# Norms' sums as products with a matrix of ones: root and reciprocal on 256 columns, no spread

## The reference, cut to what matters

```python
EPS = 1e-6
def rmsnorm(x, g):
    xf = x.astype(jnp.float32)
    y = xf * lax.rsqrt(jnp.mean(xf * xf, axis=-1, keepdims=True) + EPS)
    return (y * g.astype(jnp.float32)).astype(x.dtype)
```

## Time and profile before

| | |
|---|---|
| median of three runs | 2409.51 us |
| the profiled execution | 2409.11 us |
| its span | 2407.3 us |
| mean granted clock of TensorE | 0.988 |
| TensorE busy | 98% |
| VectorE busy | 81% |
| ScalarE busy | 63% |
| mean DMA rate | 259 GB/s |

### The profile page before, as it was taken

The page is one execution under the profiler, slowest core; times in us unless marked ns, Lnnn a source line. Parts: engine busy times, 40 slices in busy tenths (PEclk is TensorE's granted clock), DMA queues, the critical chain, the costliest instruction groups (busy, mean ns, idle before and its releaser), DMA issues.

```text
span 2407.3 us, 39686 instructions
## 1 busy us (share of the span) xinstructions
PE 2355.6 (98%) x14994; PEld 2023.5 (84%) x14994; DVE 1944.8 (81%) x2671; ACT 1519.8 (63%) x2074; POOL 0.8 (0%) x6
## 2 busy tenths in 40 slices
PE   8999999999999999999999999998999999999998
PEld 7999999999877777777777777776999999999998
DVE  6756877986588998989898989897796877887664
ACT  5655443545477878878787878786645553645552
POOL 0000000000000000000000000000000000000000
PEclk9999999999999999999999999999999999999999
DMA  9443778545579998989898999997323668323440
GB/s 370 166 155 141 291 299 340 216 192 228 210 272 357 343 366 334 366 335 364 336 363 336 365 342 358 354 352 299 140 106 131 223 241 332 141 106 141 178 156 18
DMA packets 88271, 623.69 MB, mean 259 GB/s; under 512 B 9764, under 2 KB 11464, under 8 KB 13384
## 3 DMA queue, kind: packets, MB, share of 16 engines
q1 hardware_dynamic: 87600, 621.28, 67.8%
q10 hardware_dynamic: 536, 0.53, 0.1%
HBM read 620.72 MB, written 1.05 MB: 258 GB/s over the span
## 4 chain that ended last, share of the span: by engine, by line
PE 90%; DVE 5%; ACT 2%; issue 1%; DMA 0%; SPq 0%; ACTq 0%; DVEq 0%
PE bank L653 14%; PE bank L655 14%; PE bank L654 14%; PE bank L673 10%; PE bank L677 10%; PE bank L674 10%; PE bank L874 3%; PE bank L873 3%; PE bank L871 3%; DVE ring_r L1707 2%; PE bank L1072 1%; PE bank L1218 1%; PE bank L1083 1%; DVE ring L1692 1%; PE bank L982 1%
## 5 line engine op out<-in xcount | busy, mean ns | idle before, releaser
L1707 DVE TENSOR_TENSOR ring_r<-ring,ring_r 128x1024 fp32r<-128x1024 f32 x402 | 489.5, 1222 | 183.2 <-ACT ring_r L1295 182.7
L1295 ACT ACTIVATE ring_r<-ring 128x1024 fp32r<-128x1024 f32 x402 | 423.1, 1056 | 306.9 <-PE bank L677 134.3
L673 PE MATMUL bank<-XH,ring_r 128*128 128x256 f32 x2000 | 493.0, 284 | 1.8 <-DVE ring_r L1707 1.8
L674 PE MATMUL bank<-XH,ring_r 128*128 128x256 f32 x2000 | 490.6, 283 | 0.0
L2174 DVE TENSOR_TENSOR ring_r<-ring,Z_r 128x1024 fp32r<-128x1024 f32 x336 | 409.1, 1224 | 44.8 <-ACT Z_r L1549 44.7
L2174 DVE TENSOR_TENSOR ring_r<-ring,mhat_r 128x1024 fp32r<-128x1024 f32 x336 | 406.5, 1220 | 35.3 <-ACT mhat_r L1549 34.0
L1549 ACT ACTIVATE Z_r<-ring 128x1024 fp32r<-128x1024 f32 x336 | 355.0, 1060 | 100.1 <-PE bank L655 100.0
L1549 ACT ACTIVATE mhat_r<-ring 128x1024 fp32r<-128x1024 f32 x336 | 355.2, 1061 | 89.4 <-PE bank L655 86.3
L673 PEld LDWEIGHTS bank<-XH,ring_r 128*128 128x128 f32 x2000 | 383.7, 192 | 3.1 <-DVE ring_r L1707 2.6
L674 PEld LDWEIGHTS bank<-XH,ring_r 128*128 128x128 f32 x2000 | 383.8, 192 | 0.1
L654 PE MATMUL bank<-ring_r,xn_r 128*96 128x512 f32 x896 | 351.6, 392 | 0.0
(11 more groups left out here) (351 smaller groups left out, 3638.3 us busy)
## 6 DMA issues: line engine op xcount, KB each, us to landing
ring<-in_experts SPq DMA_DIRECT2D x336, 1024.0 KB, 6.8
ring<-in_stream SPq DMA_DIRECT2D x245, 1024.0 KB, 7.3
ring<-in_stream SPq DMA_DIRECT2D x8, 512.0 KB, 6.1
xT<-in_xT SPq DMA_DIRECT2D x2, 512.0 KB, 4.6
mhat<-in_memT SPq DMA_DIRECT2D x1, 1024.0 KB, 16.7
swap<-in_early SPq DMA_DIRECT2D x1, 1024.0 KB, 19.2
swap<-in_late SPq DMA_DIRECT2D x1, 1024.0 KB, 10.2
out_T<-xn SPq DMA_DIRECT2D x8, 128.0 KB, 2.0
```

The lines of the kernel that those rows point to most:

```text
L673: pe.matmul(dst, hi[:, a], x_hi(kb), start=(n == 0), stop=False)
L674: pe.matmul(dst, lo[:, a], x_hi(kb), start=False, stop=False)
L1295: act.activation(wh(Q), raw(Q), ACT.Copy).then_inc(sems["whi"], 1)
L1707: dve.tensor_tensor(raw(Q, ring_r), raw(Q), wh(Q).bitcast(F32), ALU.subtract).then_inc(sems["wlo"], 1)
```

## The change

The sums are products with a matrix of ones as weights and the squares as the moving operand, one product of 256 columns for each block instead of two of one column. The result is in 256 columns on all partitions at once. Root and reciprocal run on 128x256, in a new tile `rroot`, and `norm_apply` reads that tile instead of a bank. The spread and its bank are gone from the plan. Norm 6 keeps the columns, norm 8 its own form. Of the filling products of the exposed norms, two stand before the sums and two behind the root; the one before the spread is gone.

```diff
+        rroot = sb("rroot", [P, 2, S])
...
         G.plan("nrm0", 1)
-        G.plan("spread0", 1)
...
         def plan_ffn(i, ni):
             G.plan(f"nrm{ni}", 1)
-            G.plan(f"spread{ni}", 1)
...
-                    for t in range(NT):
-                        mm = pe.matmul(bank[G.bank(key)][:, t:t + 1], sqb(i, kb)[:, t * P:(t + 1) * P], ones[:, 0:1],
-                                       start=(n == 0 and t == 0), stop=(kb == KB - 1), skip_group_check=True)
-                G.filled(mm, key)
-
-            def norm_spread(i):
-
-                key = f"spread{i}"
-                G.wait_free(pe, key)
-                if i in EXPOSED:
-                    keep_busy(key, 1)
-                W(pe, "rc", i)
-                for t in range(NT):
-                    mm = pe.matmul(bank[G.bank(key)][:, t * P:(t + 1) * P], rcol[:, i % 2, t:t + 1].to_broadcast([P, P]),
-                                   ident, start=True, stop=True)
+                    if i == 6:
+                        for t in range(NT):
+                            mm = pe.matmul(bank[G.bank(key)][:, t:t + 1], sqb(i, kb)[:, t * P:(t + 1) * P], ones[:, 0:1],
+                                           start=(n == 0 and t == 0), stop=(kb == KB - 1), skip_group_check=True)
+                    else:
+                        mm = pe.matmul(bank[G.bank(key)][:, 0:S], ones, sqb(i, kb), start=(n == 0), stop=(kb == KB - 1))
                 G.filled(mm, key)
                 if i in EXPOSED:
-                    G.wait_drained(pe, f"nrm{i}")
-                    keep_busy(f"nrm{i}", 2)
+                    G.wait_drained(pe, key)
+                    keep_busy(key, 2)
...
-            proj_f("f.u", 0, "f.u", between=lambda m: norm_spread(1) if m == 2 else None)
+            proj_f("f.u", 0, "f.u")
...
-                G.drained(act.activation(rcol[:, i % 2, :], bank[G.bank(key)][:, 0:NT], ACT.Sqrt, scale=1.0 / D, bias=eps),
-                          key)
+                dst, n = (rcol[:, 0, :], NT) if i == 6 else (rroot[:, i % 2, :], S)
+                G.drained(act.activation(dst, bank[G.bank(key)][:, 0:n], ACT.Sqrt, scale=1.0 / D, bias=eps), key)
...
-                dve.reciprocal(rcol[:, i % 2, :], rcol[:, i % 2, :]).then_inc(sems["rc"], 1)
-
-            def norm_apply(i, src=xT, dst=xn, hold=False):
-                key = f"spread{i}"
-                G.wait_full(dve, key)
-                g = gcol(i)
+                r = rcol[:, 0, :] if i == 6 else rroot[:, i % 2, :]
+                dve.reciprocal(r, r).then_inc(sems["rc"], 1)
+
+            def norm_apply(i, src=xT, dst=xn):
+                if i == 8:
+                    G.wait_full(dve, "spread8")
+                else:
+                    W(dve, "rc", i)
+                r, g = bank[G.bank("spread8")][:, 0:S] if i == 8 else rroot[:, i % 2, :], gcol(i)
                 for kb in range(KB):
-                    dve.scalar_tensor_tensor(out=dst[:, kb, :], in0=src[:, kb, :], scalar=g(kb),
-                                             in1=bank[G.bank(key)][:, 0:S], op0=ALU.mult, op1=ALU.mult)\
-                        .then_inc(sems["xn"], 1)
+                    dve.scalar_tensor_tensor(out=dst[:, kb, :], in0=src[:, kb, :], scalar=g(kb), in1=r,
+                                             op0=ALU.mult, op1=ALU.mult).then_inc(sems["xn"], 1)
                 W(dve, "xn", i, KB)
-                if not hold:
-                    G.drained(dve.memset(tiny[:, 255:256], 0.0), key)
```

More of the change, by code:

```diff
@@ L407, in build @@
         G.plan("nrm0", 1)
-        G.plan("spread0", 1)
-        for k, n in (("f.q", 4), ("f.f", 1), ("f.k", 4), ("line", 1), ("f.S", 4), ("nrm1", 1), ("f.v", 2), ("f.u", 2), ("spread1", 1), ("f.u2", 2),
+        for k, n in (("f.q", 4), ("f.f", 1), ("f.k", 4), ("line", 1), ("f.S", 4), ("nrm1", 1), ("f.v", 2), ("f.u", 2), ("f.u2", 2),
                      ("f.vv", 2), ("f.pT", 4), ("f.gm", 4), ("f.pv", 4), ("f.res", 8)):
@@ L415, in plan_mem @@
         def plan_mem(l, i):
-            for k, n in ((f"m{l}.k", 4), (f"nrm{i}", 1), (f"m{l}.k4", 4), (f"spread{i}", 1),
+            for k, n in ((f"m{l}.k", 4), (f"nrm{i}", 1), (f"m{l}.k4", 4),
                          (f"m{l}.q", 8), (f"m{l}.S", 4), (f"m{l}.v", 4),
@@ L431, in build @@
         G.plan("nrm4", 1)
-        G.plan("spread4", 1)
         for k, n in (("o.q", 4), ("o.k", 4), ("o.bm", 4), ("o.SA", 4), ("o.v", 2), ("o.SB", 4), ("o.h", 4),
@@ L441, in build @@
         for l in range(2):
-            for k, n in ((("nrm10", 1), ("spread10", 1)) if l else ()) + ((f"b{l}.hf", 4), (f"b{l}.hq", 4), (f"b{l}.rq", 4), (f"b{l}.rk", 4),
+            for k, n in ((("nrm10", 1),) if l else ()) + ((f"b{l}.hf", 4), (f"b{l}.hq", 4), (f"b{l}.rq", 4), (f"b{l}.rk", 4),
                          (f"b{l}.rot", 4), (f"b{l}.hi", 2), (f"b{l}.rS", 4)):
@@ L458, in build @@
         G.plan("nrm12", 1)
-        G.plan("spread12", 1)
         xnb = lambda kb: xn[:, kb, :]
@@ L779, in norm_sums @@
                         W(pe, "sq", i, kb + 1)
-                    for t in range(NT):
-                        mm = pe.matmul(bank[G.bank(key)][:, t:t + 1], sqb(i, kb)[:, t * P:(t + 1) * P], ones[:, 0:1],
-                                       start=(n == 0 and t == 0), stop=(kb == KB - 1), skip_group_check=True)
-                G.filled(mm, key)
-            def norm_spread(i):
-                key = f"spread{i}"
-                G.wait_free(pe, key)
-                if i in EXPOSED:
-                    keep_busy(key, 1)
-                W(pe, "rc", i)
-                for t in range(NT):
-                    mm = pe.matmul(bank[G.bank(key)][:, t * P:(t + 1) * P], rcol[:, i % 2, t:t + 1].to_broadcast([P, P]),
-                                   ident, start=True, stop=True)
+                    if i == 6:
[4 more added lines that the diff above has]
+                        mm = pe.matmul(bank[G.bank(key)][:, 0:S], ones, sqb(i, kb), start=(n == 0), stop=(kb == KB - 1))
                 G.filled(mm, key)
                 if i in EXPOSED:
-                    G.wait_drained(pe, f"nrm{i}")
-                    keep_busy(f"nrm{i}", 2)
-            def norm(i):
-                norm_sums(i)
-                norm_spread(i)
+                    G.wait_drained(pe, key)
+                    keep_busy(key, 2)
             def head_norm_sums(i, sq):
@@ L845, in ffn @@
             def ffn(i, ni, inst):
-                norm(ni)
+                norm_sums(ni)
                 have_hi, have_lo = split_ready(inst)
@@ L892, in _ @@
             pe.wait_ge(const_in, 16)
-            norm(0)
+            norm_sums(0)
             proj_f("f.q", 0, "f.q", have=split_ready("f"), paired=True)
@@ L953, in mem_attention @@
                 norm_sums(ni)
-                proj_f(f"m{l}.k", 1, f"m{l}.k", mh, ml, between=lambda m: norm_spread(ni) if m == 1 else None)
+                proj_f(f"m{l}.k", 1, f"m{l}.k", mh, ml)
                 for j in range(2):
@@ L992, in _ @@
             ffn(0, 3, "ffn0")
-            norm(4)
+            norm_sums(4)
             proj_f("o.q", 0, "o.q", have=split_ready("o"), paired=True)
@@ L1179, in _ @@
                 if l:
-                    norm(10)
+                    norm_sums(10)
                 rq, rk, rv, hq, kk, hi = fm(zs(0)), fm(zs(1)), zs(2), fm(zs(4)), fm(zs(8)), zs(6)
@@ L1275, in _ @@
                 ffn(l + 1, 9 + 2 * l, f"ffn{l + 1}")
-            norm(12)
+            norm_sums(12)
         @block.scalar
@@ L2264, in _ @@
                 if l == 0:
-                    norm_apply(8, hold=True)
+                    norm_apply(8)
                     x_low("b0", 0)
```

## The result

The changed kernel takes 2416.93 us (median of 11 runs, 2415.07 to 2418.34), the kernel before, beside it, 2409.34 (11 runs, 2408.11 to 2410.75). The ratio is 1.003, 95% interval 1.0022 to 1.0038: 7.6 us slower. The prediction had the sign, and its range held the time; its value was 2421.5, so the loss is 7.6 us where 12.2 were forecast. The profiled execution took 2415.67 us.

The account below looks back on a forecast made before the run. TensorE was taken to bound the kernel; exposed norms +6.35, hidden norms -1.6 and clock +7.5 gave +12.2 us on 2409.11, so 2421.4, stated as 2421.5 for the median; range of 8 in 10 2412 to 2427.

Parts of the forecast that it names:

- What bounds the kernel: Whole span: TensorE, busy 98% of 2407.3 us; a microsecond of its work or waiting is one of the result.
- The reciprocal's term: VectorE's reciprocal widened from 2 to 256 columns: 2.0 us, ends 0.48 and 2.3, in place of 0.17.
- the rival (below 1.3): Cheap wide reciprocal on VectorE, 0.48 us, deciding below 1.3: faster, 2403.2 us; chance 0.09.
- The root and the sums: Exposed norms: wider root +0.12 us, 0 to +0.2; sums 0, but 0.1 won in norm 4.
- +1.18: Cost in us forecast for each of the exposed norms 3, 4, 9 and 11, before norm 4's 0.1 for sums.
- Norms 10 and 12: Exposed norms where the clock is low: reciprocal less 1.40, so 0.6 us each, 1.2 together.
- The hidden norms: Norms 1, 2 and 5, beside projections: -0.4, -0.6 and -0.6 us, together -1.6, the longer reciprocal covered.
- The clock: Projections behind norms 3, 4, 9, 10, 11: one low stretch each after 2.25 us idle, 1.5 us, together +7.5.
- the prediction's own sign: Granted clock of 0.50 instead of 1.00 in the 1 us slices behind norms 3, 4, 9 and 11.
- norm 10's slice: Slice from 2040 before the change: TensorE 0.07 busy, then clock down to 0.50, costing up to 1.7 us.
- The clock holds, or in one or two norms not: Rival: same reciprocal, no low stretches, +4.75, 2413.9 us; with one or two, up to 2416.5; chance 0.15.
- Banks, new waits: PSUM bank rotation shifted by one: 0, below 1 us if not; gain products wait 0.04 us for the reciprocal.

Follow-up runs that it names:

- the parts done alone: The kernel before with the new form only in norms 3, 4, 9, 10, 11 (2418.12 us), only in 1, 2, 5 (2408.22), only in 0, 12 (2409.93).
- the widths run: The changed kernel with nine unread reciprocals of 2 to 1024 columns behind its last norm; its time does not count, 6.25 ns per column from 64 columns.
- the exposed-only kernel: The kernel before with the new form in norms 3, 4, 9, 10 and 11 alone; 2418.12 us, ratio 1.0031.
- the second look: The profile of the changed kernel with nine extra reciprocals at its end, unchanged up to the norms; its time does not count.
- the one-step root: The changed kernel with ScalarE's reciprocal square root in one 128x256 activation for root and reciprocal, except norm 6; 2402.91 us, ratio 0.9967 to the kernel before.
- hidden-only: The kernel before with the new form in norms 1, 2 and 5 alone; 2408.22 us against 2409.78, ratio 0.9992.
- ends-only: The kernel before with the new form in norms 0 and 12 alone; 2409.93 us against 2409.01, ratio 1.0004.

## Why the prediction came out as it did

**What bounds the kernel, and the sign: right.** Exposed norms pay to the end of the span, hidden ones don't; the parts done alone (+8.3, -1.6, +0.9) show it, each to about 2 us.

**The reciprocal's term: right in kind, 0.25 too large.** It is 1.75 us. The lower of the two slopes in the earlier trace rows, 6.5 ns, gave 1.8; I took 2.0, half way to the other one. The neighbours of the same shape, 0.38 to 0.5 us, were off by a factor of four, and to set them aside for the slope was right. That the slope itself came within 4% of 6.25 ns is luck. It was taken from two lines at different places of the program, 164 ns for two columns and 203 for eight. One behind the other, in the widths run, the same two widths take 165 and 182 ns: 2.8 ns for a column, which carried on to 256 columns gives 0.9 us, and that is the side of the rival (below 1.3).

The Trainium skill, "VectorE: DVE Perf Modes", section "First, the fixed hardware budget", has the reciprocal as an iterative divide with a repeat count of 8. It gives no price; the prediction's estimate from it and the clock of 0.96 GHz was 8.3 ns for a column and 2.13 us. The trace agrees that a column costs several times what it costs in a product, and not with the size: the measurement decides for 6.25 ns.

**The root and the sums: too small.** The root of 128x256 takes 0.47 us, not 0.38, and starts 0.08 later behind the last square. These 0.17 cancel most of the 0.25, so it is luck in part that +1.18 and the measured 1.11 to 1.13 lie so near.

**Norms 10 and 12.** Norm 10 cost 0.46, near its 0.6. Norm 12's -0.29 isn't the form: before, its sums lay in a low stretch from 2397.2 us, and after they don't. The old form with its sums on a full clock, and only its spread on the low one, has 3.5 to 3.6 us there (in the kernels with the new form in the hidden and in the exposed norms alone); the new one has 4.05. These +0.5 are near the forecast +0.6, which had the spread on a low clock too.

**The hidden norms: two near, one wrong.** Norms 2 and 5 gave the spread's 0.45 and no more; the 0.16 forecast for the sums of norm 2 didn't come, since they stand in the chain with 1.10 us where I had 0.86 and before had 1.02. Norm 5 was taken to be like norm 2, but its old sums stood in the chain with 0.79 us, less than the 0.86 of the new ones. In norm 1 I had subtracted TensorE's work from a chain that doesn't stay on TensorE. The chain of waits after:

```profile
62.71 1.06 ACT ring_r L1279
63.79 1.28 ACT L1291
65.08 0.47 ACT rroot L1291
...
70.67 2.86 DVE mhat L1718 x7
73.56 1.24 DVE ring_r L1691
```

and the timeline where it comes back to TensorE:

```profile
65.59 1.75 DVE L1709 RECIPROCAL rroot<-rroot 128x256 f32<-128x256 f32 x1 [0.56 <-ACT rroot L1291]
...
69.14 1.22 DVE L1834 TENSOR_REDUCE tiny<-Z 128x8 f32<-128x1024 f32 x1 [1.80 <-ACT Z L1384]
...
74.84 0.50 PE L650 MATMUL bank<-ring_r,XH 128*128 128x512 f32 x1 [0.66 <-DVE ring_r L1691]
```

The reciprocal is hidden, as forecast: VectorE still waits 1.80 us for ScalarE behind it. But the root's 0.21 lies on ScalarE, in front of everything that follows, and what TensorE saves turns into an idle time of 0.66 us for the weights that VectorE splits behind the gains. The net is +0.2, the root's growth. Before, TensorE's weight load at that place waited 0.18 us for VectorE: the two chains were within a few tenths of each other.

**The clock: the step that failed in size.** The prediction put one low stretch of 1.5 us behind each of five norms, +7.5. A stretch does cost that (1.38 and 1.48 us), but the profiled run had two, which is 2.86 us in place of 7.5, the exposed-only kernel three, the second look four: the number isn't fixed by the kernel. By the prediction's own sign, a clock of 0.50 in the slices behind norms 3, 4, 9 and 11, norm 11 alone of the four shows it in the profiled run. Two errors led to five of five. TensorE's idle time was 1.72 us, not 2.25, since the reciprocal was shorter and the filling products took 1.13 us and began later. And the argument had an end on either side, 0.86 us harmless and norm 10's slice not, and took everything between as lost. The first of these ends doesn't hold either: in three other traces the same 0.86 us at norm 4 is followed by a low stretch. With 3.3 or 3.4 us idle it is five of five, with no idle time at all none, and at 1.7 us it comes and goes. "The clock holds, or in one or two norms not", the rival with chance 0.15 and an upper end of 2416.5, came nearer to the profiled run than the forecast; the median of the runs, 2416.93, lies at the border of the two. The forecast of the whole, 12.2 where 7.6 came, was too high by about what the clock's term was too high, 4.6 us; that the two agree so well is chance, since other low stretches moved as well.

**Banks, new waits: right,** at 0 and 0.04.

What stays open: why the 1.7 us of idle time lose the clock in one norm and not in another, how much of the 7.6 us is the clock's, and what stops TensorE for 1.5 us in norm 8 of the kernel with six filling products. Also the low stretch between norms 4 and 5 is longer in several of the changed kernels, the one with the new form only at the ends among them, than in the three profiles of the old form, so it can't be a direct effect of the norms beside it.

## What to carry over

An operation on two columns that becomes one on 256 is not to be priced by other operations of the wide shape: here they were off by a factor of four. Its own slope over width is the better ground, but two very narrow rows give it badly (2.8 ns in one place, 6.5 from two, where the wide ones have 6.25); rows from 64 columns on, or a run with a few widths, settle it. A spread that looks like overhead may be the cheap side of the trade: find first an operation that does the wide step at stream speed (here root and reciprocal in one, 0.47 us), then drop the spread. And before work of one engine is subtracted from the chain, look how far behind the next engine's chain is.

## What the runs showed of the hardware

A reciprocal of fp32 on VectorE costs 6.25 ns for each further column from 64 to 1024 columns. For 256 columns it takes 1.69 us (1.75 where VectorE waited before it), four times the 0.40 us of a gain product of that size. ScalarE's 1/sqrt costs no more than its square root, 0.47 us each for 128x256 out of PSUM. The Trainium skill, "ScalarE: Activation LUTs", section "What it computes", sends `Rsqrt` to VectorE's reciprocal and a square root, because of known accuracy issues; by this kernel's rows that way is 2.2 us for 256 columns and the one function 0.47. The function used here has another name, which that section doesn't list, and no run here measures its accuracy, so whoever takes it has to look at that first.

The granted clock is a large part of what differs between runs of one kernel. Of the runs of the kernel before that stand beside the first experiments, the three with a mean granted clock of 0.985 took 2413.6 to 2413.7 us, and the four with 0.989 took 2407.4 to 2408.3. Summed over the span, and leaving out the first 18 to 21 us, for which the profile has no clock, the stretches at 1.2 GHz last 57.9 and 57.0 us in the two traces of before, 59.6 in after, 53.0 with the one-step root, 73.0 with no filling products; in the profiled runs of the hidden-only and the ends-only kernels, each 4.5 to 5 us above its own median, 73.4 and 74.2. A single trace of one of these kernels can therefore show up to 5 us that the medians don't have, more than several of the effects studied here.
